# A seven-product scheme for two quarters of the down projection in a two-layer fp32 trunk step

## The reference

```python
x = x + rms_norm(mixed, g_mix_post)
h = rms_norm(x, g_mlp_pre)
u = jnp.square(jax.nn.relu(jnp.einsum('btd,df->btf', h, w_up)))      # 1024 -> 4096
x = x + rms_norm(jnp.einsum('btf,fd->btd', u, w_down), g_mlp_post)   # 4096 -> 1024
```

## Time and profile before

| | |
|---|---|
| median of 3 runs | 1572.64 us (1571.6 to 1572.96) |
| profiled execution, first to last instruction | 1567.9 us |
| matmul instructions | 11984 |
| PE, DVE, ACT, POOL busy | 97%, 66%, 54%, 8% |
| granted TensorE clock, mean | 0.997 |

### The profile page before, as it was taken

How to read it: one execution, slowest core, us unless ns; L and a number is a source line. 1 busy time by engine, 2 the same in 40 slices (tenths; PEclk the granted TensorE clock), 3 DMA queues, 4 the chain that set the end, 5 groups by cost and what they waited for, 6 DMA issues and landing times.

```text
span 1567.9 us, 29899 instructions
## 1 busy us (share of the span) xinstructions
PE 1527.7 (97%) x11984; PEld 1456.7 (93%) x11984; DVE 1031.7 (66%) x1756; ACT 843.1 (54%) x1501; POOL 120.7 (8%) x160
## 2 busy tenths in 40 slices
PE   6999999999999999999999999999999999999996
PEld 6998789998999999999999987899889999999996
DVE  6883778765558654568778557778555675545765
ACT  7446654565455653446664465555645465534553
POOL 2220124000000000000002100320000000000000
PEclk9999999999999999999999999999999999999998
DMA  6644754553454555446544467344435555554562
GB/s 216 200 152 164 253 189 135 150 167 95 135 166 147 175 188 170 150 150 189 177 148 128 157 220 255 117 140 150 153 103 154 159 152 184 179 160 149 173 215 76
DMA packets 85541, 256.28 MB, mean 163 GB/s; under 512 B 8947, under 2 KB 26739, under 8 KB 85276
## 3 DMA queue, kind: packets, MB, share of 16 engines
q1 hardware_dynamic: 85404, 254.37, 51.1%
HBM read 242.52 MB, written 14.44 MB: 164 GB/s over the span
## 4 chain that ended last, share of the span: by engine, by line
PE 86%; DVE 8%; ACT 2%; DMA 2%; issue 1%; SPq 1%; DVEq 0%; ACTq 0%
PE ps L1078 68%; PE ps L1075 7%; PE ps L1138 3%; DVE w_rest L1404 2%; PE ps L1288 1%; PE ps L1303 1%; PE ps L1275 1%; DMA kc<-kcT 1%; DVE reg L1443 1%; ACT w_high L768 1%; DVE norm_every L1428 1%; DVE x L1447 1%; DVE s_in L1676 1%; DMA w_raw<-w 1%; PE ps L1193 0%
## 5 line engine op out<-in xcount | busy, mean ns | idle before, releaser
L1078 PE MATMUL ps<-h_high,w_rest 128*128 128x320 f32 (+1 forms) x1888 | 567.5, 301 | 2.8 <-DVE w_rest L1404 2.4
L1078 PE MATMUL ps<-h_high,w_high 128*128 128x320 f32 (+1 forms) x1888 | 558.2, 296 | 0.0
L1078 PE MATMUL ps<-h_rest,w_high 128*128 128x320 f32 (+1 forms) x1888 | 558.2, 296 | 0.0
L768 ACT ACTIVATE w_high<-w_raw 128x1024 fp32r<-128x1024 f32 x400 | 419.0, 1052 | 208.9 <-PE ps L1078 206.5
L1404 DVE TENSOR_TENSOR w_rest<-w_raw,w_high 128x1024 fp32r<-128x1024 f32 x396 | 490.5, 1244 | 55.2 <-ACT w_high L768 55.1
L1078 PEld LDWEIGHTS ps<-h_high,w_rest 128*128 128x128 f32 x1888 | 358.1, 190 | 16.7 <-issue 11.6
L1078 PEld LDWEIGHTS ps<-h_rest,w_high 128*128 128x128 f32 x1888 | 358.2, 190 | 0.5
L1078 PEld LDWEIGHTS ps<-h_high,w_high 128*128 128x128 f32 x1888 | 358.2, 190 | 0.0
L1078 PE MATMUL ps<-u_high,w_rest 128*128 128x256 f32 (+1 forms) x1024 | 304.9, 298 | 0.0
L1078 PE MATMUL ps<-u_high,w_high 128*128 128x256 f32 (+1 forms) x1024 | 303.1, 296 | 0.0
L1078 PE MATMUL ps<-u_rest,w_high 128*128 128x256 f32 (+1 forms) x1024 | 303.1, 296 | 0.0
(11 more groups left out here) (201 smaller groups left out, 1664.8 us busy)
## 6 DMA issues: line engine op xcount, KB each, us to landing
w_raw<-w SPq DMA_DIRECT2D x400, 512.0 KB, 3.6
kc<-kcT SPq DMA_DIRECT2D x16, 512.0 KB, 8.2
vc<-vc SPq DMA_DIRECT2D x16, 512.0 KB, 7.0
s_in<-s SPq DMA_DIRECT2D x8, 512.0 KB, 6.1
ss<-s_in SPq DMA_DIRECT2D x8, 512.0 KB, 5.8
bias<-rel_scratch SPq DMA_DIRECT2D x8, 512.0 KB, 5.5
rel_scratch<-rel_row SPq DMA_DIRECT2D x1, 2560.0 KB, 13.2
bias<-rel_scratch SPq DMA_DIRECT2D x8, 256.0 KB, 5.3
```

Source lines behind the costliest of these rows:

```text
L768: A.activation(whi[:, v % RING], raw[:, v % RING], ACT.Copy).then_inc(S["w_hi"], 1)
L1078: last = pe.matmul(ps[:, bank, 0:n], wt[:, slot, c, :], xt[:, c, :], **flags)
```

## The change

Quarters 2 and 3 are now done for both halves together: the order is ... U1A (2 units), OB, U1A (6 units), D1A, U2, D2, U3, D3, U0B, D0B, U1B, D1B. In U2 and U3 each block is loaded and split once and serves half A and half B. D2 and D3 (kind "J") are four pairs each. A pair makes two output tiles of both halves from two down blocks, seen as a 2 x 2 matrix (two outputs by two halves of the contraction, HC = 4 chunks each), against a 2 x 2 matrix of activations (contraction half by token half; B's 256 columns stand against A's 256 prompt columns). Winograd's form of Strassen's scheme takes seven products of 4 chunks x 3 terms = 12 matmuls. Four are 320 columns wide, three 256 (one of these has a single 320-column matmul).

Each product has a weight operand ("entry") of half a block: three are quarters of the two raw blocks, four are sums S1 to S4, made on POOL (`sums`, 128x512, serial) into raw slots 1, 2 and 3. Each entry is split by ACT (`half_high`) and DVE (`half_rest`); the rings `w_high` and `w_rest` hold 8 entries, so entry g + 8 is made after product g. The two raw blocks of a pair always lie in slots 0 and 1, and `raw_free` lets SP load them only when all seven entries of the pair before have been split. The activation combinations T1 to T4 are made on DVE during U2 and U3 (`mix`) and split on ACT and DVE (`mix_high`, `mix_rest`). DVE adds each product into the accumulators it belongs to: ten evictions a pair. PSUM banks come in two sets of four (`JB`); products 2, 5 and 6 add onto a bank whose earlier content must have been evicted (`EV_X` = 3 evictions, `EV_V`, `EV_Y`).

```diff
+U1_CUT = 2
+Q_ORDER = ((0, 1, 2, 3), (2, 3, 0, 1))
+JOINT = (2, 3)
+MIX = (0, 4, 1, 5, 2, 6, 3, 7)
+HC = KC // 2
+PRODUCTS = 7
+EVICTS = 10
+EV_X, EV_Z, EV_X2, EV_V, EV_Y, EV_V2, EV_Y_A, EV_Y_B = 3, 4, 5, 6, 7, 8, 9, 10
+ENTRIES = 2 * RING
+E_A11, E_A22, E_A12, E_S1, E_S2, E_S4, E_S3 = range(PRODUCTS)
+T4, T1, T2, T3 = range(4)
+T_SET = {T1: 1, T2: 2, T4: 3, T3: 4}
+ENTRY_AT = ((0, 0), (1, HC), (0, HC), (2, 0), (2, HC), (3, 0), (1, 0))
...
+        if kind == "J":
+            first += 8
+            return [((first + 2 * k, first + 2 * k + 1), [("J", None, k, q)]) for k in range(HC)]
+        ks = MIX if kind == "U" and q in JOINT else range(KC)
...
+    u1 = m_units("U", 1, (0,))
+    seq += [("U1A", u1[:U1_CUT]), ("OB", o_units(1)), ("U1A", u1[U1_CUT:])]
+    for name, kind, q, halves in (("D1A", "D", 1, (0,)), ("U2", "U", 2, (0, 1)), ("D2", "J", 2, (0, 1)),
+                                  ("U3", "U", 3, (0, 1)), ("D3", "J", 3, (0, 1)),
+                                  ("U0B", "U", 0, (1,)), ("D0B", "D", 0, (1,)), ("U1B", "U", 1, (1,)), ("D1B", "D", 1, (1,))):
...
+                slot = v % 2 if v in pair_of else v % RING
+                landed = S[f"j_in{slot}"] if v in pair_of else S[f"w_in{slot}"]
+                sp.dma_start(raw[:, slot].rearrange("p a b -> p (a b)"),
+                             w[loads[v]:loads[v] + 1].rearrange("o p n -> p (o n)")).then_inc(landed, 16)
+
+            def raw_free(v):
+
+                if v in pair_of:
+                    if pair_of[v] % HC == 0:
+                        sp.wait_ge(S[lo_of[v - RING][0]], lo_of[v - RING][1])
+                    else:
+                        sp.wait_ge(S["j_lo"], PRODUCTS * pair_of[v])
+                elif v - RING in pair_of:
+                    sp.wait_ge(S["j_lo"], PRODUCTS * HC * (pair_of[v - RING] // HC + 1))
+                else:
+                    sp.wait_ge(S[lo_of[v - RING][0]], lo_of[v - RING][1])
...
+            def sums(p, which):
+
+                for n in which:
+                    s1, s2, s4, s3 = (entry_source(e) for e in (E_S1, E_S2, E_S4, E_S3))
+                    a11, a12, a22 = (entry_source(e) for e in (E_A11, E_A12, E_A22))
+                    if n == 0:
+                        pool.wait_ge(S["j_in0"], 16 * (p + 1))
+                        pool.wait_ge(S["j_in1"], 16 * (p + 1))
+                        if p % HC == 0:
+                            v = min(v for v in pair_of if pair_of[v] == p)
+                            for u in (v - 2, v - 1):
+                                pool.wait_ge(S[lo_of[u][0]], lo_of[u][1])
+                        else:
+                            pool.wait_ge(S["j_lo"], PRODUCTS * p)
+                        V.tensor_tensor(s1, s3, a22, ALU.add).then_inc(S["j_sum"], 1)
+                    elif n == 1:
+                        pool.wait_ge(S["j_sum"], 4 * p + 1)
+                        V.tensor_tensor(s2, s1, a11, ALU.add).then_inc(S["j_sum"], 1)
+                    elif n == 2:
+                        pool.wait_ge(S["j_sum"], 4 * p + 2)
+                        V.tensor_tensor(s4, s2, a12, ALU.add).then_inc(S["j_sum"], 1)
+                    else:
+                        pool.wait_ge(S["j_sum"], 4 * p + 1)
+                        V.tensor_tensor(s3, s3, a11, ALU.add).then_inc(S["j_sum"], 1)
...
+                if o.kind == "J" and o.k < HC - 1:
+                    sums(o.evn + 1, range(4))
+                elif mixed_u(o) and o.h and o.k == KC - 2:
+                    sums(HC * quarter(o), range(4))
...
+            def half_high(p, i):
+
+                if i in (E_A11, E_A12, E_A22):
+                    act.wait_ge(S["j_in1" if i == E_A22 else "j_in0"], 16 * (p + 1))
+                else:
+                    act.wait_ge(S["j_sum"], 4 * p + {E_S1: 1, E_S2: 2, E_S4: 3, E_S3: 4}[i])
+                e = (PRODUCTS * (p % HC) + i) % ENTRIES
+                A.activation(half_block(whi, e), entry_source(i), ACT.Copy).then_inc(S["j_hi"], 1)
...
+                if o.k == 0:
+                    mix_high(o.l, o.tile, HC - 1, range(4))
+                for i in range(PRODUCTS):
+                    g = PRODUCTS * o.k + i
+                    act.wait_ge(S["j_done"], first + g + 1)
+                    if g + ENTRIES < PRODUCTS * HC:
+                        half_high(p + (i + ENTRIES) // PRODUCTS, (i + ENTRIES) % PRODUCTS)
...
+                        if v + RING in pair_of:
+                            for e in (2 * (v % RING), 2 * (v % RING) + 1):
+                                half_high(pair_of[v + RING] // HC * HC + e // PRODUCTS, e % PRODUCTS)
+                        else:
+                            high(v + RING)
...
+                work = ((bx, slice(0, n_a), lambda c: (uh[0][:, c, :], ul[0][:, c, :])),
+                        (bz, slice(0, n_a), lambda c: (t4_h[:, c, :], t4_l[:, c, :])),
+                        (bx, slice(0, n_a), lambda c: (uh[0][:, HC + c, :], ul[0][:, HC + c, :])),
+                        (bv, slice(0, n_b), lambda c: (uh[1][:, c, :], ul[1][:, c, :])),
+                        (by_, mix_a, lambda c: (t_high(T2, c), t2_l[:, c, :])),
+                        (bv, slice(0, n_b), lambda c: (uh[1][:, HC + c, :], ul[1][:, HC + c, :])),
+                        (by_, slice(0, n_a), lambda c: (t3_h[:, c, :], t3_l[:, c, :])))
+                for i, (bank, cols, moving_of) in enumerate(work):
+                    e = (PRODUCTS * o.k + i) % ENTRIES
+                    pe.wait_ge(S["j_lo"], PRODUCTS * p + i + 1)
+                    begins = i in (0, 1, 3, 4)
+                    if begins:
+                        take(bank)
+                    else:
+                        pe.wait_ge(S["j_ev"], EVICTS * p + {2: EV_X, 5: EV_V, 6: EV_Y}[i])
+                    for c in range(HC):
+                        if o.k == 0:
+                            if i in (0, 2, 5):
+                                pe.wait_ge(S["u_set"], u_no[o.l, i // 5, c + (HC if i else 0), o.tile])
+                            else:
+                                pe.wait_ge(S["t_lo"], n + 4 * c + {1: T4, 3: T1, 4: T2, 6: T3}[i] + 1)
+                        th, tl = moving_of(c)
+                        wh, wl = half_block(whi, e)[:, c, :], half_block(wlo, e)[:, c, :]
+                        for m, (wt, xt) in enumerate(((wl, th), (wh, tl), (wh, th))):
+                            at_cols = cols
+                            if i == 4 and c == 0 and m == 0:
+                                at_cols, xt = slice(0, n_a), t2_hz[:, 0:n_a]
+                            last = pe.matmul(ps[:, bank, at_cols], wt, xt, start=(begins and c == 0 and m == 0),
+                                             stop=(c == HC - 1 and m == 2), skip_group_check=True)
+                    last.then_inc(S["j_done"], 1)
...
+            def half_rest(p, i):
+
+                e = (PRODUCTS * (p % HC) + i) % ENTRIES
+                dve.wait_ge(S["j_hi"], PRODUCTS * p + i + 1)
+                V.tensor_tensor(half_block(wlo, e), entry_source(i), half_block(whi, e).bitcast(F32), ALU.subtract)\
+                    .then_inc(S["j_lo"], 1)
...
+                dve.wait_ge(S["u_sq"], sq_no[o.l, 1, o.k, o.tile])
+                dve.wait_ge(S["t_raw"], n + 1)
+                V.tensor_tensor(t_whole(T2, c), four, t_whole(T1, c), ALU.add).then_inc(S["t_raw"], 1)
+                dve.wait_ge(S["t_raw"], n + 2)
+                V.tensor_tensor(t_whole(T4, c), two, t_whole(T2, c), ALU.subtract).then_inc(S["t_raw"], 1)
+                V.tensor_tensor(t_whole(T3, c), three, four, ALU.subtract).then_inc(S["t_raw"], 1)
...
+                if o.k == 0:
+                    mix_rest(o.l, o.tile, HC - 1, range(4))
+                    if opens:
+                        dve.wait_ge(S["ev_d"], made[o.l, "D", 0, KC - 1, JOINT[0] - 1].evn)
+                    else:
+                        dve.wait_ge(S["j_ev"], EVICTS * p)
+                for i in range(PRODUCTS):
+                    g = PRODUCTS * o.k + i
+                    dve.wait_ge(S["j_done"], first + g + 1)
+                    done = EVICTS * p
+                    if i == 0:
+                        whole, prompt = ps[:, bx, 0:n_a], ps[:, bx, mix_a]
+                        V.tensor_tensor(a2, a2, whole, ALU.subtract).then_inc(S["j_ev"], 1)
+                        if opens:
+                            V.tensor_copy(b1, prompt).then_inc(S["j_ev"], 1)
+                            V.tensor_scalar(b2, prompt, -1.0, None, ALU.mult).then_inc(S["j_ev"], 1)
+                        else:
+                            V.tensor_tensor(b1, b1, prompt, ALU.add).then_inc(S["j_ev"], 1)
+                            V.tensor_tensor(b2, b2, prompt, ALU.subtract).then_inc(S["j_ev"], 1)
+                    elif i == 1:
+                        dve.wait_ge(S["j_ev"], done + 1)
+                        V.tensor_tensor(a2, a2, ps[:, bz, 0:n_a], ALU.add).then_inc(S["j_ev"], 1)
+                    elif i == 2:
```

(30 more changed lines are left out.)

266 lines of the change are left out of this document (207 added, 59 removed), and 3 rows, old and new, of the table seq.

## The result

The changed kernel is slower: a median of 1632.28 us over four runs (1630.84 to 1635.0) against 1572.12 for the kernel before, measured beside it (1570.53 to 1572.96). The ratio is 1.0386, with a 95% interval of 1.0371 to 1.0402. The forecast was 1619.0, in a range from 1590 to 1642. The profiled execution spans 1633.2 us against the 1567.9 of before, 65.3 more. All times here are of undisturbed executions; a single one, of the eighth experiment's kernel, took 5127 us and is left out.

What follows compares the result with a forecast made beforehand. PE was taken to bound the kernel. Per quarter, 12.9 us waits, 2.6 sums and 1.3 clock less 5.6 saved gave 11.2; four quarters plus 1.8 gave +46.4, so 1614.3, carried to 1619.0 us; range 1590 to 1642.

Steps and rivals of the forecast that it cites:

- What bounds the kernel: MLP phases: pure PE time, each matmul removed is worth its pace, as long as nothing makes PE wait.
- rival 4: Products don't run at the present tiles' pace; 10 ns on each of 1344 matmuls would add 13 us; 3%.
- The wait inside a quarter: Pairs 1 and 2: DVE's half rest waits for the landing before evictions; PE stands 2.4 us each, 4.8 per quarter.
- The wait at the start of a quarter: Pair 0: PE stands 5.97 us for T4's remainder, then 2.15 before product 2; together 8.1 us per quarter.
- POOL's sums: Fetched pairs: POOL's sums block DVE operations, 0.86 us per pair, 2.6 per quarter; ends zero and 8.6.
- rival 3: Blocking and clock at their high ends, each sum of POOL winning against DVE: 1635 to 1650; 15%.
- PE's clock: Quarter's start: one fall to 1.2 GHz after the 6 us stand, 1.3 us per quarter; ends 0 and 2.6.
- Small change at U2: Half B's first U tile waits for DVE's last chunks of `h_rest`: 0.9 us, twice 1.8; ends 0 and 3.
- The sum: Whole kernel: 11.2 us more per quarter, four times 44.6, with 1.8 at U2 +46.4 us, giving 1619.0.
- rival 1: D2 and D3: the landing is hidden and the PE cut stands, 1550 us; 6%.
- rival 2: Only the start of a quarter stalls, PE's lag in pair 0 letting later loads catch up: +10, 1583; 6%.
- hidden "by totals": In a pair, DVE's 9.3 to 10.2 us and ACT's 4.3 fit under 11.4 of PE by totals, not by order.

Runs made afterwards that it cites:

- the eighth experiment: Changed kernel with late half rests and sums cut, plus T4's remainder and product 0's evictions first at a quarter's start: 1577.3 us, ratio 1.0026.
- both causes out: Seventh experiment: changed kernel with half rests moved behind products 2 to 5 and POOL's sums cut to 8 elements: 1567.54 us, ratio 0.9972.
- the second experiment: Changed kernel with the next pair's half rests made later only inside a quarter, pair 0 keeping its old order: 1633.4 us.
- the first three experiments: Changed kernel with half rests later: throughout, 1607.33 us; only inside a quarter, 1633.4 us; throughout with the quarter's start put in order, 1615.97 us.
- Without the sums: Changed kernel with POOL's four sums per pair cut to 8 elements each, waits and order kept: 1612.2 us, ratio 1.0252.
- The dummy matmuls: Changed kernel with 34 and 24 unread matmuls put into the two stands at each quarter's start: 1622.73 us, ratio 1.0333.
- the pairs without loads: Changed kernel without the loads of pairs 1 to 3, whose products use old blocks, sums made in full: 1589.93 us, ratio 1.0111.
- The best order run here: Changed kernel with earlier loads, the quarter's start in order and DVE's half rests spread behind nearly every product, sums in full: 1575.66 us, ratio 1.0031.
- late halves: Changed kernel with ACT's and DVE's halves of the next pair moved behind products 2 to 5: 1607.33 us, ratio 1.0213.
- the kernel without block products: Changed kernel with its new phase order, but D2 and D3 as plain tiles with as many matmuls as before: 1574.18 us, ratio 1.0010.

## Why the prediction was right, point by point

**What bounds the kernel.** Right. PE time removed is worth its pace: with both causes out, four quarters take 195.6 us, 9.2 less than before, and pairs of 11.39 us stand in the trace where nothing delays them, just as worked out. The matmuls of the products run at 146.7 and 120.0 ns, so rival 4 is out.

**The wait inside a quarter.** Right in mechanism and size: 2.4 us were worked out, eight stands of 2.10 to 2.86 with a mean of 2.41 us came (2.57 if counted as the forecast does, from the time at which the matmul was due to its start; the profile counts idle time from the end of the last matmul), all behind a half rest that waits for ACT and a landing. Pair 3 had 0.04, as said. But the step left out something: the stand is not the price. Taking it away alone gave nothing (the second experiment), since the sums behind it then come to bear. The forecast was right about this kernel and would have been wrong about its repair, as the expectations of the first three experiments were.

**The wait at the start of a quarter.** The first stand was put at 5.97 us and is 5.59 to 5.66, or 5.8 counted from the due time; DVE was 0.2 us ahead of the plan. The second was put at 2.15 and is 4.17. Here two errors met. Without the sums it is 0.96 (1.3 from the due time), so the chain behind the landing was put 0.9 us too long: neighbouring short operations of DVE start 0.34 us apart and not 0.42, and product 2 was due later, since PE's last three matmuls in front of it ran at half clock. And the sums make three remainders take 4.4 instead of 1.26 us, and all of this, 3.2 us, shows in the stand. It belongs to the next term, that of the sums.

**POOL's sums.** The mechanism held, its size was off. I took 0.86 us per fetched pair, 2.6 per quarter. The stands that the sums make come to 3.7: 3.2 at the entry, and 0.5 in front of products 5 and 6 of pairs 1 and 2, where after has five short stands in all four quarters (0.02 to 0.56 us). The step that failed is "one block of 0.86 us per fetched pair": in the rows each of the three remainders at the entry waits for a whole sum, while pairs 1 and 2 hide nearly all of theirs behind the stand for the landing. As it turned out, each sum gets in ahead of DVE's next operation at the entry, which was the condition of rival 3, but its price does not show in pairs 1 and 2, so the time is between the forecast and that rival. The price of the sums by experiment is larger, 5.3 us per quarter, because 1.4 us of half clock go with them. The Trainium skill, "SBUF — State Buffer", section "Who interferes with whom", calls the shared port an exclusive lock; the trace agrees, with 0.42 us remainders at 1.44 to 1.50 and evictions from PSUM at 0.41 throughout.

**PE's clock.** Too small by 2.8 us per quarter, the largest miss. I took one fall of 1.3 us per quarter for the 6 us stand. Matmuls at half clock cost 2.1 to 5.3 us, mean 3.5, and the first ones behind the two stands of the entry another 0.6. The granted clock is 0.50 from 550.7 to 560.9, since the second stand follows before the clock is back, and in some pairs it fell after the short stands too (twice in D3 of layer 0, at 690.6 and 707.7). The dummy matmuls gave back 2.4 of it. By the Trainium skill, "TensorE: Matmul & The Clock Gate", section "Why this matters for your kernels", idle gaps between bursts bring the half clock; the trace agrees for the long stand in all four quarters, and for the short ones in some.

**Small change at U2.** 0.9 us each was right (0.97 twice); U3 has another 0.3 each, which I had at nothing.

**The sum.** Per quarter 14.7 us over the old time instead of 11.2. Counted from the due times, the mean extra of 20.35 us splits into 12.2 for the landing (12.9 forecast), 3.7 for the sums (2.6), 4.1 for the clock (1.3) and 0.3 that no term had: 1.1 more from the sums, 2.8 more from the clock, 0.7 less from the landing. So part of the closeness is luck, since the last of these offsets some of the others. The four quarters come to 14.2 us more than forecast (58.8 against 44.6). The medians differ by 60.2 us where 46.4 were forecast, 13.8 more.

**The rivals.** The landing isn't hidden (rival 1), and pairs 1 and 2 do stall (rival 2): their rows are above. What I called hidden "by totals" does fit by totals (the pairs without loads show it), and by order it doesn't, as the prediction said. The best order run here brings the new scheme to within 0.3% of the old one. The seven products are worth 22.6 us of PE, and no kernel run here that makes its sums in full came out ahead of the kernel before.

What stays open: whether the last few us of pair 1 could be had with more raw slots, or with the sums on another engine, wasn't tried, and why the kernel of the eighth experiment is 10 us slower than the seventh is not shown.

## What to carry to other kernels

When a schedule waits in place for a load, take the wait out on paper and go through the same stretch again: what it covered comes next, and here it was as large. Where two engines shut each other out, count their time as one engine's time, and place it operation by operation: 9.9 of 11.4 us fits by totals and still stalls when it may start only at a landing. An algorithm with fewer matmuls moves its saving into additions and splits; where PE was the only full engine, it is these that must fit under a shorter PE time.

## What the runs showed of the hardware

What POOL's sums cost depends on the order of DVE's work beside them: 20 us with the old order and 40 us with late halves, with the sums unchanged. DVE operations with both inputs in SBUF, one after another while POOL runs its sums, each wait for the sum that is running: 0.68 us half rests become 1.2 to 1.8, 0.42 us remainders 1.44 to 1.50. Where evictions from PSUM stand between them, as in pairs 1 and 2 without loads, a half rest takes 0.68 to 1.04 us beside the sums. POOL pays as well: the second to fourth sums there take 1.63 to 1.82 us in D2 of layer 1, against 1.29 alone.

The granted clock fell in after also in phases with the same work as before. Window of 12 us ahead of U1A, of the kernel before and then of the kernel after (columns as above):

```profile
300.00:312.00 12.00, 9.87 (x84) 9.69 (x84) 11.47 (x24) 5.50 (x11) 0.00 (x0) 1.00 0.62 183
```

```profile
300.00:312.00 12.00, 9.87 (x72) 9.69 (x71) 10.30 (x19) 5.85 (x12) 0.00 (x0) 0.86 0.58 189
```

PE is busy 9.87 of 12 us in both, and the clock is 1.00 in one and 0.86 in the other. The kernel without block products has a fall at that place too, and the one with late halves alone has none, though the phases up to there are the same in all of them. So it is not the change by itself that makes it. No run here says what does.

Fewer bytes bought nothing: DMA moved 222.7 MB against 256.3 of before, with 336 weight loads against 400, and the time went up. What PE stood for was the landing of single blocks, 3.6 us from their issue, and POOL's sums, and not the traffic.
